# Linear attention's level masks moved from a stage of their own into GpSimd, beside the first steps of the attention

## The reference, cut to what matters

```python
def direction(f_pre, lb_dir, reverse):
    z = f_pre.astype(jnp.float32)
    log_f = jnp.logaddexp(jnp.log(lb_dir), jnp.log1p(-lb_dir) + jax.nn.log_sigmoid(z))
    k = -jnp.expm1(log_f)
    ...                                # chunked scan: o = q . decayed sum of k v, causal mask inside
```

## Time and profile before

| | us |
|---|---|
| median of 3 runs | 3666.77 (3664.34 to 3669.01) |
| the profiled execution, its own time | 3664.36 |
| its span from first to last instruction | 3662.6 |
| TensorE busy in the span | 3160.6 (86%) |
| VectorE, ScalarE, GpSimd busy | 1414.0, 898.6, 156.4 |

### The profile page before, as it was taken

The page is one execution under the profiler, slowest core; times in us unless marked ns, Lnnn a source line. Parts: engine busy times, 40 slices in busy tenths (PEclk is TensorE's granted clock), DMA queues, the critical chain, the costliest instruction groups (busy, mean ns, idle before and its releaser), DMA issues. The chain is left out here.

```text
span 3662.6 us, 35498 instructions
## 1 busy us (share of the span) xinstructions
PE 3160.6 (86%) x14334; PEld 2305.1 (63%) x14334; DVE 1414.0 (39%) x2162; ACT 898.6 (25%) x1446; POOL 156.4 (4%) x220
## 2 busy tenths in 40 slices
PE   7995777998898885888882798999998899999997
PEld 7784754445676572332221777788776778888886
DVE  3124856874434334111113755531215233333334
ACT  3324334442324210000001131012222222222121
POOL 0000011000000000111110300000000000000000
PEclk9997979999899997999896899999999989999999
DMA  3110000002120045999995022211112111111112
GB/s 92 48 45 9 1 13 1 1 1 109 47 97 12 29 164 210 419 421 420 412 380 180 24 66 48 72 47 47 37 55 86 35 46 46 52 46 49 50 47 74
DMA packets 138914, 369.97 MB, mean 101 GB/s; under 512 B 45632, under 2 KB 59584, under 8 KB 112640
## 3 DMA queue, kind: packets, MB, share of 16 engines
q1 hardware_dynamic: 128400, 346.93, 25.8%
q0 software_dynamic: 9216, 16.80, 1.2%
q10 hardware_dynamic: 1152, 4.19, 0.3%
HBM read 352.66 MB, written 32.79 MB: 105 GB/s over the span
## 5 line engine op out<-in xcount | busy, mean ns | idle before, releaser
L2435 PE MATMUL moe_ph<-moe_wgu,moe_rowsT 128*64 128x512 f32 x1024 | 262.4, 671 | 70.0 <-DMA moe_wgu<-in_moe_w_up_dram 40.9
L516 PE MATMUL mlp_ps<-mlp_high,mlp_w_cut 128*128 128x512 f32 x1024 | 317.1, 391 | 6.0 <-DVE mlp_w_cut L431 6.0
L516 PE MATMUL mlp_ps<-mlp_w_cut,mlp_hidden_high 128*128 128x512 f32 x1024 | 315.2, 389 | 0.0
L431 DVE TENSOR_TENSOR m_w_cut<-m_w_raw,m_w_cut 128x512 fp32r<-128x512 f32 (+1 forms) x92 | 94.3, 1029 | 455.0 <-ACT m_w_cut L427 454.7
L431 DVE TENSOR_TENSOR mlp_w_cut<-mlp_w_raw,mlp_w_cut 128x1024 fp32r<-128x1024 f32 x64 | 78.3, 1225 | 399.0 <-ACT mlp_w_cut L427 398.5
L2435 PEld LDWEIGHTS moe_ph<-moe_wgu,moe_rowsT 128*64 128x64 f32 x1024 | 83.5, 154 | 228.7 <-issue 203.4
L427 ACT ACTIVATE m_w_cut<-m_w_raw 128x512 fp32r<-128x512 f32 (+1 forms) x92 | 76.4, 835 | 605.9 <-PE m_gates_ps L516 196.4
L516 PEld LDWEIGHTS mlp_ps<-mlp_high,mlp_w_cut 128*128 128x128 f32 x1024 | 193.3, 189 | 46.7 <-DVE mlp_w_cut L431 6.4
L516 PEld LDWEIGHTS mlp_ps<-mlp_w_cut,mlp_hidden_high 128*128 128x128 f32 x1024 | 192.2, 188 | 39.9
L516 PE MATMUL mlp_ps<-mlp_low,mlp_w_cut 128*128 128x512 f32 x512 | 200.0, 391 | 0.0
L516 PE MATMUL mlp_ps<-mlp_w_cut,mlp_hidden_low 128*128 128x512 f32 x512 | 199.2, 389 | 0.0
(11 more groups left out here) (525 smaller groups left out, 5887.8 us busy)
## 6 DMA issues: line engine op xcount, KB each, us to landing
moe_wgu<-in_moe_w_gate_dram SPq DMA_DIRECT2D x64, 1024.0 KB, 19.4
moe_wgu<-in_moe_w_up_dram SPq DMA_DIRECT2D x64, 1024.0 KB, 25.8
moe_wd<-in_moe_w_down_dram SPq DMA_DIRECT2D x64, 1024.0 KB, 19.7
mlp_w_raw<-in_w_ff_dram SPq DMA_DIRECT2D x64, 512.0 KB, 3.3
m_w_raw<-in_w_in_dram SPq DMA_DIRECT2D x48, 256.0 KB, 2.8
mix_w_raw<-in_w_in_dram SPq DMA_DIRECT2D x40, 256.0 KB, 2.6
m_w_raw<-in_w_in_dram SPq DMA_DIRECT2D x20, 512.0 KB, 3.5
x_w_raw<-in_x_w_kv_dram SPq DMA_DIRECT2D x16, 512.0 KB, 3.6
```

What stands on the lines that cost most here:

```text
L431: nc.vector.tensor_tensor(part(s, 1).bitcast(F32R), raw(s), part(s, 0), ALU.subtract).then_inc(low_ready, 1)
L516: ins = nc.tensor.matmul(ps[:, b, :r.shape[-1]], l, r, start=(k == 0 and sw is high and wh == 0), stop=(k == job.nk - 1 and sw is low))
L2435: ins = self.nc.tensor.matmul(self.ps_h[r, i].rearrange("p (i n) -> p i n", i=2), self.rowsT[:, i, k, r], self.wgu[:, w * self.parts + h, ...
```

## The change

The ten iotas, the ten transposes and the three VectorE instructions go, with their blocks. GpSimd makes the masks in `hgrn`'s own block: for each width a memset to 1 and two affine selections leave 1 only within the groups of w (the group's block on the diagonal). Then, from the widest down, each level's mask minus the next narrower one leaves the pairs in different halves, and for level 0 the identity is subtracted. The last instruction raises `masked`, for which VectorE waits once, ahead of its first `copy_predicated`. The mask tensor moves from `mix_first`'s allocation into `hgrn`'s.

The bounds move into the side task of the projection: VectorE takes the difference as its first side step (piece 0), ScalarE makes both sigmoids at piece 8. Their two blocks go.

```diff
--- before.py
+++ after.py
@@ -932,48 +932,13 @@
 
 
 
-def level_masks(c, ctx):
-
-    nc = c.nc
-    mask = sbuf(ctx, nc, "mask", [P, MASKED, P])
-    with ExitStack() as tmp:
-
-        half = sbuf(tmp, nc, "mask_half", [P, MASKED, P])
-        base = sbuf(tmp, nc, "mask_base", [P, MASKED, P])
-        halfT = sbuf(tmp, nc, "mask_halfT", [P, MASKED, P])
-        baseT = sbuf(tmp, nc, "mask_baseT", [P, MASKED, P])
-        with nc.Block() as block:
-            @block.gpsimd
-            def _(pool):
-                for l in range(MASKED):
-                    w = 2 << l
-                    nc.gpsimd.iota(base[:, l], [[w, P // w], [0, w]], base=0, channel_multiplier=0,
-                                   allow_small_or_imprecise_dtypes=True)
-                    nc.gpsimd.iota(half[:, l], [[w // 2, 2 * P // w], [0, w // 2]], base=0,
-                                   channel_multiplier=0, allow_small_or_imprecise_dtypes=True)
-        items = [[src[:, l]] for src in (base, half) for l in range(MASKED)]
-
-        def out(n, bank, copy):
-            return copy((baseT if n < MASKED else halfT)[:, n % MASKED], bank[:, :P])
-
-        turn(c, "masks", items, out)
-        with nc.Block() as block:
-            @block.vector
-            def _(dve):
-                do = c.chain("vector", dve)
-                do(nc.vector.tensor_tensor(base[:], base[:], baseT[:], ALU.is_equal))
-                do(nc.vector.tensor_tensor(half[:], half[:], halfT[:], ALU.not_equal))
-                do(nc.vector.tensor_tensor(mask[:], base[:], half[:], ALU.mult))
-    return mask
-
-
 def view(t, offset, dims):
 
     a = t[:] if not isinstance(t, bass.AP) else t
     return bass.AP(tensor=a.tensor, offset=a.offset + offset, ap=[list(a.ap[0])] + [list(d) for d in dims])
 
 
-def hgrn(c, inputs, q, keep, key, values, lb, lb1, mask, queries, out, lies):
+def hgrn(c, inputs, q, keep, key, values, lb, lb1, queries, out, lies):
 
 
 
@@ -989,10 +954,10 @@
         s = lambda n, shape: sbuf(ctx, nc, f"hg_{n}", shape)
         whole, mine = lies("hg_whole", [P, 2, 2, T // 2], 48), lies("hg_mine", [P, 2, T], 56)
         pairT, kdT = lies("hg_pairT", [P, 2, NT, P], 64), lies("hg_kdT", [P, 2, NT, P], 72)
-        state = s("state", [P, 2, NT, P])
+        state, mask = s("state", [P, 2, NT, P]), s("mask", [P, MASKED, P])
         ps = psum(ctx, nc, "hg_ps", 8)
         per_slot = lambda n: [c.sem(f"hg_{n}{a}") for a in range(2)]
-        prepared = c.sem("hg_prepared")
+        prepared, masked = c.sem("hg_prepared"), c.sem("hg_masked")
         seeded, product, keys_grown, gathered, queries_grown, placed, corners = [per_slot(n) for n in (
             "seeded", "product", "keys_grown", "gathered", "queries_grown", "placed", "corners")]
         merged, turned, copied, update, stepped, summed, evacuated = [per_slot(n) for n in (
@@ -1033,6 +998,21 @@
             def _(sp):
                 with nc.allow_non_contiguous_dma("small parameters"):
                     c.relays = s5_relay(sp, inputs, c.relaid, c.relay)
+
+            @block.gpsimd
+            def _(pool):
+
+                do = c.chain("gpsimd", pool)
+                for l in range(MASKED):
+                    w = 2 << l
+                    t = mask[:, l].rearrange("p (n w) -> p n w", w=w)
+                    do(nc.gpsimd.memset(mask[:, l], 1.0))
+                    for step, first, way in ((-w, 1, 1), (w, w, -1)):
+                        do(nc.gpsimd.affine_select(out=t, in_=t, compare_op=ALU.is_gt, fill=0.0, base=first,
+                                                   pattern=[[step, P // w], [0, w]], channel_multiplier=way))
+                for l in range(MASKED - 1, 0, -1):
+                    do(nc.gpsimd.tensor_tensor(mask[:, l], mask[:, l], mask[:, l - 1], ALU.subtract))
+                nc.gpsimd.tensor_tensor(mask[:, 0], mask[:, 0], c.ident[:], ALU.subtract).then_inc(masked, 1)
 
             @block.scalar
             def _(act):
@@ -1108,6 +1088,8 @@
                     nc.vector.tensor_tensor(decays(a, h, l + 1), pairs[:, :, :, 0], pairs[:, :, :, 1],
                                             ALU.mult).then_inc(merged[a], 1)
                     if l < MASKED:
+                        if a == 0 and r == 0 and l == 0:
+                            dve.wait_ge(masked, 1)
                         dve.wait_ge(placed[a], (MASKED + 1) * r + l + 1)
                         nc.vector.copy_predicated(
                             pairT[:, a], mask[:, l].bitcast(I32).unsqueeze(1).to_broadcast([P, NT, P]),
@@ -1228,8 +1210,10 @@
 class RopeTables(Side):
 
 
-    def __init__(self, c, mla_in, posi, cos, sin, kn, small, gains, room):
+
+    def __init__(self, c, mla_in, posi, cos, sin, kn, small, gains, room, bounds):
         self.c, self.mla_in, self.posi, self.cos, self.sin, self.kn = c, mla_in, posi, cos, sin, kn
+        self.bounds, self.bound_ready = bounds, c.hold_sem("lb_ready")
 
         self.rstd, self.under = small[:, 0:2], small[:, 2]
         self.gain, self.other = gains
@@ -1254,6 +1238,13 @@
 
     def scalar_steps(self, act):
         nc = self.c.nc
+        lbl, lb, lb1 = self.bounds
+        while self.piece < KD:
+            yield None
+        act.wait_ge(self.bound_ready, 1)
+        do = self.c.chain("scalar", act)
+        do(nc.scalar.activation(lb1, lb, ACT.Sigmoid, scale=-1.0))
+        do(nc.scalar.activation(lb, lb, ACT.Sigmoid))
         while self.piece < 2 * KD:
             yield None
         act.wait_ge(self.emptied["scalar"], NT)
@@ -1280,6 +1271,8 @@
     def vector_steps(self, dve):
         nc = self.c.nc
         do = self.c.chain("vector", dve)
+        lbl, lb, lb1 = self.bounds
+        nc.vector.tensor_tensor(lb, lbl[:, 0], lbl[:, 1], ALU.subtract).then_inc(self.bound_ready, 1)
         do(nc.vector.tensor_copy(self.pos, self.posi))
         for j in range(HALF):
             freq = float(np.float32(1.0) / np.float32(ROPE_BASE ** (j / HALF)))
@@ -1665,24 +1658,11 @@
                 norm_split(c, "mix", x, pair, gain, NT, room[:, :3 * D], fetch=fetch,
                            arrived=[(c.x_in[m], 16) for m in range(NT)], gain_in=(c.gain_in, 16))
                 rope = RopeTables(c, mla_in, posi[:, :, 0], cos[:], sin[:], kn[:], scales[:], (qg[:], kg[:]),
-                                  gate[:].rearrange("p m v -> p (m v)"))
+                                  gate[:].rearrange("p m v -> p (m v)"), (lbl[:], lb[:], lb1[:]))
                 project(c, "mix_in", stream, jobs, side=rope)
 
-            mask = level_masks(c, hg)
-            with nc.Block() as block:
-                @block.vector
-                def _(dve):
-                    do = c.chain("vector", dve)
-                    do(nc.vector.tensor_tensor(lb[:], lbl[:, 0], lbl[:, 1], ALU.subtract))
-            with nc.Block() as block:
-                @block.scalar
-                def _(act):
-                    do = c.chain("scalar", act)
-                    do(nc.scalar.activation(lb1[:], lb[:], ACT.Sigmoid, scale=-1.0))
-                    do(nc.scalar.activation(lb[:], lb[:], ACT.Sigmoid))
-
             queries = hT[:, 0:4].rearrange("p (a d) t -> p a d t", a=2)
-            hgrn(c, a, q, logf, key, values, lb, lb1, mask, queries, values, lies)
+            hgrn(c, a, q, logf, key, values, lb, lb1, queries, values, lies)
             mla_prepare(c, a, mla_in[:], rope, qn[:], (qga[:], qgb[:], kvg[:]), onorm[:], values[:], gate[:], hT,
                         x[:].rearrange("p m d -> p (m d)"), qT[:], kT[:], v[:], rq[:])
         head_pairs(c, "mla_attn", qT, kT, v,
```

## The result

The changed kernel took 3646.79 us in the median of five runs (3642.22 to 3650.54), beside 3664.34 for the kernel before (3660.66 to 3669.01). The ratio is 0.9949, with a 95% interval of 0.9938 to 0.9961. On 3664.34 us that is 18.7 us, between 14.3 and 22.7. The two medians are 17.55 apart.

A forecast was written before the change was run, and what follows sets the result against it. The stretch between projection and attention, one engine working at a time, was taken to be on the path; other terms were taken as 0. From a 3666.77 us median, 13.75 goes: 3653.0, range 3646 to 3660.

The forecast's parts named there:

- The stretch: Between projection and attention, from 292.88 to 306.63, all work and block ends go: 13.75 us.
- the block end: Clearing semaphores and entering the attention's block stays: 1.14 us, with 0.9 more gain or 1.1 less allowed.
- GpSimd's chain: Twenty mask instructions in the attention's block: 10.0 us, upper end 23.2, hidden because VectorE needs the first mask after 25.9.
- VectorE beside GpSimd: Attention's three seed products may each wait for a GpSimd instruction, 3.3 us at most, within slack: cost 0.
- The bounds in the projection: VectorE's difference (0.17) and ScalarE's table load and sigmoids (1.70, in a 4.68 gap) are covered: cost 0.
- TensorE's clock: In the attention's level steps the clock's rise may shift three steps either way, 3.9 us; taken as 0.
- the 2.3 for the runs around the median: Whole-kernel term of the forecast's range: runs lie 2.3 us around the median.
- own range: Whole kernel: the forecast's narrower range, 3648 to 3658 us, at 0.84.
- Masks late: Rival: at VectorE's first masked placing, slow GpSimd selections cause a 51 us wait; kernel 37 slower, 3704; chance 0.04.
- The clock giving the gain back: Rival: TensorE stays at half clock seven level steps more, 9.1 us return, gain 4.7, time 3662.1; chance 0.06.
- uncovered in the projection: Rival: ScalarE's sigmoids delay a cut that TensorE needs in the projection; 1.9 us come back, 3654.9; chance 0.04.
- The entry to the attention's long block: Rival: entering this block needs something the mask stages hid; up to 13.75 us stays idle, 3666.8; chance 0.02.

The follow-up runs named there:

- masks_thrice: The changed kernel with GpSimd making the masks three times over; ratio 0.9981 (0.9971 to 0.9991) to the kernel before.
- before_busy: The kernel before with 120 idle TensorE products ahead of and between the attention's first products and in the preparation; ratio 0.9994 (0.9984 to 1.0005).
- masks_only: The changed kernel with the bounds kept in their two blocks between projection and attention; 13.6 us (8.8 to 18.3) faster than the kernel before.
- again3: The changed kernel timed once more with no edit, its fourth set; ratio 0.9956 (0.9939 to 0.9974) to the kernel before.
- bounds_only: The kernel before with the bounds made beside the projection and the old mask stage kept; its time can't be told from no change.
- busy_short: The changed kernel with idle TensorE products, 20 before the attention's first product, 38 before its second, none in the preparation; ratio 0.9950 (0.9936 to 0.9963).
- after_busy: The changed kernel with the same 120 idle TensorE products that were also put into the kernel before; ratio 0.9965 (0.9953 to 0.9978).

## Why the prediction was right or wrong

**The stretch.** Right. It was forecast as 13.75 and is 13.93 to 13.95 in the four profiles of the changed kernel; the difference is the block end, 0.94 for 1.14. No table load came ahead of the scaling. That agrees with the Trainium skill's "ScalarE: Activation LUTs" ("Table sets: the hidden batching unit"), by which the cheap functions are in every set.

**GpSimd's chain.** Right in what it decides: 11.4, between the 10.0 forecast for the chain alone and the 13.6 with the wait for three products. Beside VectorE's seed products two pairs took 2.40 and 1.25, in place of 0.74 and 0.68 where VectorE is idle (masks_thrice, 323.54 and 324.61); without that the chain is 9.2. Selections by level, in pairs, after the 295.01 start:

```profile
295.27 1.48 POOL L1011 TENSOR_SCALAR_AFFINE_SELECT hg_mask<-hg_mask 128x128 f32<-128x128 f32 x2
...
297.09 1.12 POOL L1011 TENSOR_SCALAR_AFFINE_SELECT hg_mask<-hg_mask 128x128 f32<-128x128 f32 x2
...
298.54 0.88 POOL L1011 TENSOR_SCALAR_AFFINE_SELECT hg_mask<-hg_mask 128x128 f32<-128x128 f32 x2
```

That is 0.74, 0.56 and 0.44 each for runs of 2, 4 and 8. The dearest selection of an undisturbed pair stays under the 1.09 that I had for a bound. The memsets took 0.20, the subtractions 2.06 for four, close to the 457 ns each of the earlier trace rows.

**VectorE beside GpSimd.** Right, and visible. The pair of selections at 299.75 took 2.40, while the pair of that width at 323.54 in masks_thrice, with VectorE idle, took 0.74. VectorE's first seed product ran from 299.49 to 300.71 beside it. The two products after it took 2.55 in place of 2.35. Most of the bill was GpSimd's. The Trainium skill's "SBUF — State Buffer" ("SBUF: two separate sides") says that a VectorE instruction with two operands in SBUF and a GpSimd one that reads SBUF hold the shared ports in turn, each for its whole length. The pair's 1.66 more, beside products of 1.2, is of that size. By the rule VectorE could have lost as much; here it lost 0.2. All of it lay in slack on both sides.

**The bounds in the projection.** Right. ScalarE's rows around piece 8, for the earlier trace rows:

```profile
68.79 0.62 ACT L427 ACTIVATE mix_w_cut<-mix_w_raw 128x512 fp32r<-128x512 f32 x1
69.43 1.28 ACT L1246 ACT_TABLE_LOAD   x1
70.73 0.21 ACT L1246 ACTIVATE lb<-lb 128x8 f32<-128x8 f32 x1
70.97 0.21 ACT L1247 ACTIVATE lb<-lb 128x8 f32<-128x8 f32 x1
74.11 0.63 ACT L427 ACTIVATE mix_w_cut<-mix_w_raw 128x512 fp32r<-128x512 f32 x1 [2.93 <-PE mix_in_ps L516]
```

and TensorE's waits within the projection, for the earlier trace rows:

```profile
PE mix_in_ps L516 <- DVE mix_w_cut L431: 3.7, 1, 3.7
```

1.75 of ScalarE's 4.68 went, and 2.93 were left. TensorE still waited once.

**The size.** This is where the prediction was off. The step that failed is the one on TensorE's clock, "The rise can come three steps earlier or three later than here: 3.9 us either way. I take 0", with the 2.3 for the runs around the median. The clock's share was priced for the level steps alone and put at nothing for every later stage, and the runs' spread was taken from three runs. The own range was also narrower than its terms: 3.9 + 0.9 + 2.3 below 3653.0 is 3645.9, not 3648. Of the 6.2 us between 3653.0 and 3646.79, 2.4 are the kernel before (3664.34 in this set, 3666.77 in the three runs) and 3.8 the gain (17.55 for 13.75).

In the two profiles the preparation gave 3.8, the rest behind it 2.5, and the level steps, the only part that was priced, 1.7; the projection took 1.2 back. Windows of the preparation in the kernel before, then in the changed one, from about its start (500.27 and 485.79):

```profile
500.00:520.00 20.00, 12.06 (x24) 4.70 (x24) 7.12 (x22) 6.26 (x10) 6.28 (x9) 0.64 0.18 56
520.00:540.00 20.00, 18.10 (x56) 8.68 (x56) 9.74 (x25) 8.96 (x18) 5.49 (x11) 0.76 0.00 0
540.00:560.00 20.00, 15.24 (x54) 7.74 (x52) 12.18 (x29) 8.22 (x16) 5.89 (x10) 0.74 0.00 0
```

```profile
487.00:507.00 20.00, 12.07 (x21) 4.96 (x21) 6.39 (x21) 5.07 (x8) 5.37 (x9) 0.57 0.18 57
507.00:527.00 20.00, 17.65 (x61) 8.61 (x60) 11.26 (x30) 9.92 (x20) 6.62 (x14) 0.83 0.00 0
527.00:547.00 20.00, 15.21 (x65) 8.14 (x66) 13.48 (x32) 10.47 (x21) 6.45 (x12) 1.00 0.00 1
```

The clock is 0.64, 0.76, 0.74 in the one and 0.57, 0.83, 1.00 in the other. The stage's length followed: 106.31 and 102.56. The code for it is the same in all 16 kernels here but for the idle products, and one window over the whole stage gives its mean clock in each profile:

```
mean granted clock   preparation      profiles
0.93                 99.20            before_busy
0.85                 102.56           after
0.84                 103.88, 103.98   masks_only, again3
0.81 to 0.82         106.0 to 106.6   before and eight others
0.78                 109.43, 109.57   bounds_only, busy_short
```

The sixteenth, after_busy, took 107.40 at 0.84, with TensorE busy for 88.2 us by its idle products, where before_busy had 78.7. The stages after the preparation, the same in all, took between 3049.4 and 3059.8. And whole runs go with the clock: of the kernel before, the 15 later runs with a mean clock of 0.927 or 0.928 took 3668.0 on average, the 23 with 0.931 or 0.932 took 3659.7.

So the first comparison held a removed stretch of 13.95 and a few microseconds of clock, by luck in the change's favour; later sets gave 15.0, 13.6 and 16.1. What makes the clock rise earlier in one execution than in another stays open. So does whether 1 or 2 us beyond the stretch belong to the change: the pooled 13.7 to 17.5 allows for them, and no stage shows them in all profiles.

**The rivals.** Masks late is a true mechanism with the threshold that I gave (25.9, measured 25.8), but the chain is far from it. The clock giving the gain back did not happen; it moved the other way in the first set by chance. Nothing came uncovered in the projection. The entry to the attention's long block cost no more than before (0.94 for 1.14).

## What to carry to other kernels

A stretch in which the blocks stand in a row with one engine at work each can be priced from the timeline alone, to 0.2 us here: last end before it to first start behind it, minus one block end. Whether it was worth it can't be read from one pair of profiles once the gain is below some 0.5%, which is how far 23 runs of one kernel lay apart here (19.3 us): compare the stages, and run the same program again before giving a surplus a cause. After such a stage is gone, look at what the next block starts with: here eight scalings that nobody needed yet were worth about half as much as the change (8.0 beside 15.6).

## What the hardware showed that was not expected

- TensorE's clock fell to half in the level steps even when 84 idle products had held it at full up to their start (1.00, 0.82, 0.50 in the windows of after_busy), and ahead of them after a wait of 2.62 us (busy_short). Filling the idle stretch ahead of this stage bought nothing in the stage itself.
- One stage with the same instructions took from 99.2 to 109.6 us, and but for one profile its length follows the mean granted clock, from 0.93 to 0.78.
- An idle product of 128x128 in this type shows as two matmuls in the trace, and 64 of them took 14.46 us at full clock. That was 3 to 4 us more than the stretch they were to fill.
- A pair of GpSimd's selections over runs of 4 took 1.12 us beside an idle VectorE and 3.46 beside its level steps (masks_thrice, 318.54). GpSimd lost more than VectorE, whose product at 319.81 there kept its 1.20.
